# Loading the modulation weights and the first weight units between the two token halves of x

## The reference, cut to what matters

```
def rms_norm(x, g):
    x32 = x.astype(jnp.float32)
    y = x32 * lax.rsqrt(jnp.mean(x32 * x32, axis=-1, keepdims=True) + EPS)
    return (y * g.astype(jnp.float32)).astype(x.dtype)

def ada_params(cvec, w, b):
    m = jax.nn.silu(cvec) @ w + b
    return jnp.split(m, 3, axis=-1)

def modulate(x, g, shift, scale):
    return rms_norm(x, g) * (1.0 + scale) + shift
...
        shift, scale, gate = ada_params(c, ada_w[i], ada_b[i])
        ...
        h = modulate(x_lat, norm_g[i], shift[:, None, :], scale[:, None, :])
        ...
            proj = h @ w_in
```

## Time and profile before

| What | us |
|---|---|
| three runs | 2718.04, 2719.57, 2719.70 |
| median of the three | 2719.57 |
| the profiled execution | 2720.78 |
| its span in the profile, first to last instruction | 2718.8 |
| PE busy | 2655.6 (98%) |
| DVE busy | 1675.7 (62%) |
| ACT busy | 1017.9 (37%) |
| POOL busy | 1011.1 (37%) |

### The profile page before, as it was taken

One profiled execution on the slowest core, in us unless ns is written; L12 is line 12 of the kernel. 1 busy time (PEld: TensorE's weight loads), 2 busy tenths in 40 slices (PEclk: granted clock), 3 DMA queues, 4 the chain that ended last, 5 costly groups with the idle time before them and its releaser, 6 DMA issues.

```text
span 2718.8 us, 39199 instructions
## 1 busy us (share of the span) xinstructions
PE 2655.6 (98%) x16062; PEld 2189.9 (81%) x16062; DVE 1675.7 (62%) x1847; ACT 1017.9 (37%) x1392; POOL 1011.1 (37%) x612
## 2 busy tenths in 40 slices
PE   8999999999999999999999999999999999999997
PEld 5888878887788887788888888888777888888885
DVE  6496669867844457544556676666878443344446
ACT  4342247753433333544442223332334222222222
POOL 0254243114688853222121111111144654444552
PEclk9999999999999999999999999999999999999998
DMA  7211710034222232111121111111132111121112
GB/s 247 72 32 39 263 47 1 1 101 127 68 62 57 53 116 85 47 47 47 47 58 40 40 34 38 40 40 40 32 93 63 55 47 47 47 63 55 55 34 98
DMA packets 248541, 175.26 MB, mean 64 GB/s; under 512 B 6064, under 2 KB 236848, under 8 KB 247216
## 3 DMA queue, kind: packets, MB, share of 16 engines
q1 hardware_dynamic: 246928, 170.22, 20.3%
q10 hardware_dynamic: 1440, 2.59, 0.3%
HBM read 164.40 MB, written 8.39 MB: 64 GB/s over the span
## 4 chain that ended last, share of the span: by engine, by line
PE 68%; issue 13%; DVE 9%; POOL 4%; ACT 3%; DVEq 2%; SPq 1%; DMA 0%; POOLq 0%; ACTq 0%
PE PS L2619 10%; PE PS L2621 10%; PE PS L2620 10%; PE PS L2219 10%; PE PS L2221 9%; PE PS L2220 9%; POOL Wlo L629 3%; DVE qR L1709 2%; ACT exp L1070 1%; DVE acol L1757 1%; PE PS L2723 1%; PE PS L2730 1%; PE PS L2532 1%; PE PS L2808 1%; DVE qz L1713 1%
## 5 line engine op out<-in xcount | busy, mean ns | idle before, releaser
L629 POOL TENSOR_TENSOR Wlo<-Wraw,Whi 128x1024 fp32r<-128x1024 f32 (+1 forms) x140 | 342.0, 2443 | 989.1 <-ACT Whi L844 972.7
L2219 PE MATMUL PS<-Bh,Whi 128*128 128x512 f32 x1184 | 472.4, 399 | 6.3 <-DVE Bl L1501 2.8
L2221 PE MATMUL PS<-Bh,Wlo 128*128 128x512 f32 x1184 | 461.8, 390 | 0.0
L2220 PE MATMUL PS<-Bl,Whi 128*128 128x512 f32 x1184 | 461.2, 390 | 0.0
L2219 PE MATMUL PS<-Hh,Whi 128*128 128x512 f32 x672 | 266.0, 396 | 3.8 <-POOL Wlo L629 1.2
L2219 PEld LDWEIGHTS PS<-Bh,Whi 128*128 128x128 f32 x1184 | 222.1, 188 | 59.0 <-DVE Bl L1501 6.9
L2221 PE MATMUL PS<-Hh,Wlo 128*128 128x512 f32 x672 | 261.8, 390 | 0.0
L2221 PEld LDWEIGHTS PS<-Bh,Wlo 128*128 128x128 f32 x1184 | 222.2, 188 | 47.7
L2220 PEld LDWEIGHTS PS<-Bl,Whi 128*128 128x128 f32 x1184 | 222.5, 188 | 44.2 <-issue 0.7
L2220 PE MATMUL PS<-Hl,Whi 128*128 128x512 f32 x608 | 236.8, 389 | 0.0
L2166 DVE TENSOR_TENSOR X<-X,PS 128x1024 f32<-128x1024 f32 x56 | 68.3, 1221 | 204.7 <-PE PS L2621 203.9
(11 more groups left out here) (459 smaller groups left out, 5927.7 us busy)
## 6 DMA issues: line engine op xcount, KB each, us to landing
Wraw<-in_w_in SPq DMA_DIRECT2D x64, 512.0 KB, 4.0
adarow<-in_ada_rows SPq DMA_DIRECT2D x32, 512.0 KB, 6.8
Wraw<-in_odd_w_in SPq DMA_DIRECT2D x32, 512.0 KB, 5.0
Wraw<-in_w_up SPq DMA_DIRECT2D x32, 512.0 KB, 4.0
Wraw<-in_w_down SPq DMA_DIRECT2D x28, 512.0 KB, 4.2
Wraw<-in_even_w_in SPq DMA_DIRECT2D x24, 512.0 KB, 3.9
adaW<-in_ada_in SPq DMA_DIRECT2D x8, 1024.0 KB, 11.6
Wraw<-in_even_w_out SPq DMA_DIRECT2D x14, 512.0 KB, 3.6
```

Source lines behind the costliest of these rows:

```text
L629: pool.tensor_tensor(Wlo[:, slot, 0:tiles, :], Wraw[:, slot, 0:tiles, :], Whi[:, slot, 0:tiles, :].bitcast(F32), ALU.subtract).then_inc(lo ...
L2219: mm(out, Whi[:, u % 2, k, :], hi[:, k, c], start=(k == 0), stop=False)
L2220: mm(out, Whi[:, u % 2, k, :], lo[:, k, c], start=False, stop=False)
L2221: return mm(out, Wlo[:, u % 2, k, :], hi[:, k, c], start=False, stop=(k == KT - 1))
```

## The change

SP issues the first half of x, pieces 0 and 1, units 0 and 1, the second half of x, and then pieces 2 to 7. The other engines follow that order:

- ACT squares the first half only, takes its root (L926), copies the first rows, splits both units, and then squares the second half, two squares before each of the first two high parts.
- DVE inverts the first root, makes the first columns, tiles (0, 0) and (1, 0), and only then the second half's sums, its root, tiles (0, 1) and (1, 1), and the second columns.
- PE makes the products of tiles (0, 0) and (1, 0) before the second half's sum. That sum is four products instead of two, the last two squares going in without an addition. The second modulation rows follow, then product (0, 1), the second columns, product (1, 1).

The number of matmuls for `Hh` and `Hl` stays; six filler products go. `FIRST_HALVES` lists the new order of the halves. Context squares and the context's load wait for all six of the sum's products. From channel tile 2 on all is as before.

```diff
-        for h in range(2):
+
+        def x_half(h):
+
             c = slice(h * 512, h * 512 + 512)
...
-        unit_at(0, 0, w_in0)
-        for t in range(8):
-            if t == 2:
-                unit_at(1, P, w_in0)
...
+        x_half(0)
+        ada_piece(0)
+        ada_piece(1)
+        unit_at(0, 0, w_in0)
+        unit_at(1, P, w_in0)
+        x_half(1)
+        for t in range(2, 8):
+            ada_piece(t)
+        sp.wait_ge(sem("xsq_read"), 6)
...
+        for n in range(KT):
+            square_half(n)
+        x_roots(0)
         rows_out(0)
+        split(0, 0, 16)
         split(1, 1, 16)
+        for n in range(2):
+            square_half(KT + 2 * n)
+            square_half(KT + 2 * n + 1)
+            high_half(n)
+        for n in range(4, KT):
+            square_half(KT + n)
+        x_roots(1)
         act.dma_start(chan[:, :], nW["chan_dft"]).then_inc(sem("chan_loaded"), 16)
-        for j in range(4):
+        rows_out(1)
+        high_half(2)
+        high_half(3)
+        for j in range(1, 4):
...
+        def second_sum():
+
+            for n, tile in enumerate((4, 8, 10, 11)):
+                if n < 2:
+                    pe.wait_ge(sem("xsq_added"), n + 3)
+                else:
+                    pe.wait_ge(sem("xsq_ready"), n + 13)
+                mm(bank(5), ones, xsq[:, tile, :], start=(n == 0), stop=(n == 3)).then_inc(sem("xsq_read"), 1)
...
         modulation_columns(0)
         keep_running(3)
+        first_products(0, 0)
+        first_products(1, 0)
+        second_sum()
         modulation_rows(1, (0,))
         keep_running(4)
-        for j in range(1, 4):
+        modulation_rows(1, (1,))
+        first_products(0, 1)
+        modulation_columns(1)
+        first_products(1, 1)
+        for j in range(2, 4):
             first_products(2 * j - 2, 0)
-            modulation_rows(j, (1,) if j == 1 else (0, 1))
+            modulation_rows(j)
```

More of the change, by code:

```diff
@@ L282, in build @@
         (c0 + 1024, c0 + 1280, c0 + 2560, c0 + 3328, c0 + 3584, c0 + 3840, t0 + 52736))]
+    FIRST_HALVES = [(0, 0), (1, 0), (0, 1), (1, 1)] + [(k, h) for k in range(2, KT) for h in range(2)]
     ROWS = 6
@@ L904, in act_program, with square_half, x_roots @@
         act.activation(small[:, 8:10], bank(0, 2), ACT.Exp).then_inc(sem("act_setup"), 1)
-        for n in range(2 * KT):
+        def square_half(n):
             h, k = n // KT, n % KT
             act.wait_ge(sem(f"slot_loaded{4 * h + k // 2}"), 16)
-            if n == 12:
-                act.wait_ge(sem("xsq_read"), 1)
-            act.activation(xsq[:, n % 12, :], X[:, k, h * 512:h * 512 + 512], SQUARE).then_inc(sem("xsq_ready"), 1)
-        split(0, 0, 16)
-        for h in range(2):
-            act.wait_ge(sem("xsq_read"), 2 * h + 2)
+            if n == 8:
+                act.wait_ge(sem("xsq_read"), 2)
+            act.activation(xsq[:, k + 4 * h, :], X[:, k, h * 512:h * 512 + 512], SQUARE).then_inc(sem("xsq_ready"), 1)
+        def x_roots(h):
+            act.wait_ge(sem("xsq_read"), (2, 6)[h])
             act.activation(Rx[:, h * 512:h * 512 + 512], bank(4 + h), SQRT, bias=EPSC, scale=1.0 / D).then_inc(sem("x_root"), 1)
@@ L937, in act_program @@
             if k < 4:
-                act.wait_ge(sem("xsq_read"), 4)
+                act.wait_ge(sem("xsq_read"), 6)
             else:
@@ L1575, in scaled_half @@
         def scaled_half(n):
-            k, c = n // 2, slice(n % 2 * 512, n % 2 * 512 + 512)
+            k, h = FIRST_HALVES[n]
+            c = slice(h * 512, h * 512 + 512)
             stt(tnx[:, n % 4, :], X[:, k, c], A0[:, k:k + 1], Rx[:, c], ALU.mult, ALU.mult).then_inc(sem("x_tn"), 1)
         def low_half(n):
-            k, c = n // 2, slice(n % 2 * 512, n % 2 * 512 + 512)
+            k, h = FIRST_HALVES[n]
+            c = slice(h * 512, h * 512 + 512)
             dve.wait_ge(sem("x_hi"), n + 1)
@@ L1584, in add_fours @@
         def add_fours(n):
-            a = 4 * (n % 3)
+            a = 4 * min(n, 1)
             for b in (0, 2):
@@ L1590, in add_fours @@
             tt(xsq[:, a, :], xsq[:, a, :], xsq[:, a + 2, :], ALU.add).then_inc(sem("xsq_added"), 1)
-        for n in range(4):
-            add_fours(n)
+        add_fours(0)
+        add_fours(1)
         root_to_scale(0)
-        root_to_scale(1)
-        modulation_columns(0)
-        for j in range(4):
+        modulation_columns(0)
+        scaled_half(0)
+        scaled_half(1)
+        low_half(0)
+        low_half(1)
+        add_fours(2)
+        dve.wait_ge(sem("xsq_ready"), 14)
+        tt(xsq[:, 8, :], xsq[:, 8, :], xsq[:, 9, :], ALU.add).then_inc(sem("xsq_added"), 1)
+        root_to_scale(1)
+        scaled_half(2)
+        scaled_half(3)
+        low_half(2)
+        low_half(3)
+        modulation_columns(1)
+        for j in range(1, 4):
             n = 4 * j
@@ L2313, in pe_program @@
         keep_running(5)
-        for h in range(2):
-            for j in range(2):
-                n = 2 * h + j
-                if n:
-                    keep_running(2 if n == 1 else 3)
-                pe.wait_ge(sem("xsq_added"), n + 1)
-                mm(bank(4 + h), ones, xsq[:, 4 * (n % 3), :], start=(j == 0), stop=(j == 1)).then_inc(sem("xsq_read"), 1)
+        for n in range(2):
+            if n:
+                keep_running(2)
+            pe.wait_ge(sem("xsq_added"), n + 1)
+            mm(bank(4), ones, xsq[:, 4 * n, :], start=(n == 0), stop=(n == 1)).then_inc(sem("xsq_read"), 1)
+        def second_sum():
[5 more added lines that the diff above has]
+                mm(bank(5), ones, xsq[:, tile, :], start=(n == 0), stop=(n == 3)).then_inc(sem("xsq_read"), 1)
         def column_tiles(out, W, sem_done):
@@ L2342, in modulation_columns @@
                 pe.wait_ge(sem("m_ready"), j - 1)
-            if j == 0:
-                pe.wait_ge(sem("x_root"), 2)
+            if j < 2:
+                pe.wait_ge(sem("x_root"), j + 1)
             for t in range(2):
```

8 lines of the change are left out of this document (5 added, 3 removed).

## The result

| What | before, us | after, us |
|---|---|---|
| median of seven runs each | 2719.57 | 2728.11 |
| lowest and highest run | 2718.04, 2720.44 | 2725.28, 2735.61 |
| the profiled execution | 2720.78 | 2725.73 |
| its span | 2718.8 | 2723.8 |
| PE busy | 2655.6 | 2654.9 |

The changed kernel is slower by 0.36%: the ratio of the times is 1.0036, with a 95% interval of 1.0026 to 1.0045. The forecast was 2726.6 and the range 2721.5 to 2731.0. One slow run of the kernel before, of 14047.14 us, lies among those beside units_plain, rows_first, score_fill and rows_fill, and counts in no comparison.

A forecast was written before the change was run, and what follows sets the result against it. TensorE sets the time after the opening, so an opening delay reaches the end: 44.25 - 37.70 = +6.55 us, plus 0.5 for the clock, +7.05 on the 2719.57 median, giving 2726.6 us; range 2721.5 to 2731.

The forecast's parts named there:

- the mark: Start of the second modulation columns on DVE: 37.70 us before, 44.25 forecast; the kernel moves by what it moves.
- Landings: Opening transfers arrive in issue order: second half of x 9.5 us later, the modulation 7.3 us earlier, same total.
- First columns: First modulation columns reach DVE at 20.6 us instead of 28.49, 7.9 us ahead.
- The hold: POOL's low-part subtractions block DVE's scale operation and first scaled tile, which ends at 26.2 us instead of 22.1.
- rival 1: Opening: weight splits don't hold DVE, or come late enough; +3.7 us, total 2723.3, chance 0.19.
- The ping-pong and the second sum: DVE and ACT alternate on tiles and squares; PE's sum of the second half runs 31.6 to 35.3 us.
- From the sum to the mark: Second root 0.75, reciprocal 3.4, tile until 41.8, product group 1.4 and columns 1.0, reaching 44.25 us.
- Costed at nothing: Opening: rows of pieces 2 and 3, row copy, early products, later loads and removed fillers add 0 us.
- The clock: PE idles 5.6 us in the opening, then runs at half clock: +0.5; second fall taken as 0, 2.4 in range.
- rival 2: Opening: PE's lower clock stays or comes twice; +10.4 us, total 2730.0, chance 0.13.
- For 3: Rival: second root hidden, piece 3 sets the second columns at 35.2 us, 2.5 earlier; total 2717.1, chance 0.04.
- For 4: Rival: opening transfers share engines and land together, piece 1 and units up to 3 us later; about +10, chance 0.04.

The follow-up runs named there:

- units_plain: changed kernel with weight units 0 and 1 transferred ahead of modulation pieces 0 and 1, and ACT's splits ahead of root and rows; median 2731.98 us, ratio 1.0040.
- rows_first: kernel before with PE's modulation rows moved ahead of each round's first product in the loop over channel pairs; median 2719.87 us, ratio 0.9999.
- score_fill: kernel before with nine filler products on PE ahead of the attention stage's first ten transposes, near 382.5 us; median 2717.81 us, ratio 0.9994.
- rows_fill: kernel before with both the earlier modulation rows of rows_first and the attention-stage fillers of score_fill; median 2718.46 us, ratio 0.9994.
- fill_no_lock: changed kernel with fillers in PE's two idle stretches, and POOL writing zeros as low parts of units 0 and 1, left out of the product; median 2722.88 us.
- order_alone: kernel before with only SP's new order of transfers, the engines staying in the old order; median 2729.53 us, ratio 1.0036.
- engines_alone: changed kernel with the transfers back in the old order, so the engines' new order alone; median 2736.90 us, ratio 1.0059.
- fill: changed kernel with twelve instead of three fillers behind the first modulation columns and four behind piece 3's rows; median 2725.04 us, ratio 1.0026.
- no_lock: changed kernel with POOL writing zeros, reading nothing, as low parts of units 0 and 1, which the product leaves out; median 2724.52 us, ratio 1.0018.
- long_sum: fill with four more products of 512 columns ahead of the second half's sum, overwritten by it; median 2730.03 us, ratio 1.0038 to the kernel before.
- after_again: the changed kernel run once more with no edit, beside the kernel before; median 2727.78 us, ratio 1.0026.

## Why the prediction was right, point by point

- **What bounds, and the mark.** Right for the profiled execution, and not enough for the median. The mark moved by 6.19 us on the axis, 5.95 of it stood at 1245 us and 4.97 at the end. The medians of fill_no_lock and order_alone lie 3.6 and 10.0 above the kernel before, their marks 3.54 and 9.95 behind its own. But others don't fit as well: 8.5 for 6.83 in the changed kernel, 17.6 for 14.85 in engines_alone, 12.1 for 7.81 in units_plain. Behind the mark stand the fall at 386 us and the hold beside it, each in some executions only.
- **Landings.** Right in order and rate. First rows straight behind the sum, piece 1's rows at 17.11, unit 1's split at 20.31 and second-half squares at 21.67 are each 0.5 to 0.6 ahead of the prediction's axis (17.7, 20.9 and 22.2), as S is (0.64).
- **First columns.** 20.6 predicted, 19.96 measured: 6.58 after S, and 6.58 by the prediction.
- **The hold.** The mechanism and its size: 2.85 us were what the hold was worth in the sum (6.55 against rival 1's 3.7), 2.40 were measured by the pair fill and fill_no_lock. The first tile ended 0.5 behind POOL's splits (0.7 predicted), with 3.29 for the two tiles. With POOL only writing (no_lock) the hold was gone. The Trainium skill, "SBUF — State Buffer", section "Who interferes with whom", has a DVE instruction with two SBUF inputs and a GpSimd instruction that reads SBUF exclude each other; the traces agree, with 1.95 against 0.16 us for L1598.
- **The ping-pong and the second sum.** Sum predicted 31.6 to 35.3, measured 31.28 to 34.88. From S the start is 17.90 instead of 17.58, but two errors meet in it: without the lower clock it is 16.91 (fill), 0.67 less than summed, and the lower clock added 0.99. That the sum lies on the path, long_sum shows (3.43 for 3.6).
- **From the sum to the mark.** 12.65 predicted, 12.61 measured.
- **Costed at nothing.** Held: the rows of pieces 2 and 3 ran beside the reciprocal, the row copy was done at 39.62, ahead of the high part at 39.85.
- **The clock: the term that was mis-sized.** I took +0.5 for the first fall; it was 0.89 (30.51 against 29.62), and the low level lasted 6.8 us and not some 3. The sum without the clock was +6.55, and fill, without a fall in the opening, has +5.94. So I was 0.61 too high there and 0.39 too low for the clock, and that +7.05 came so near to the +6.83 from S is in part luck. I took 0 for a second fall, and kept 2.4 for the range. In the first changed execution it was 0; in after_again the mark was 2.63 later, 1.51 of it by the second fall and 1.12 by a later first one. That is rival 2's mechanism, with a chance of 0.13, and one of two profiled executions had it. The forecast for the like of the profiled execution (2727.8) was 2.1 too high: 0.9 of it on the axis at the mark (7.05 against 6.19, of which 0.64 is the earlier S), the rest given back behind it (6.19 to 4.97). That for the median (2726.6) was 1.5 too low. The step that failed is taking one execution's clock for the median's: the changed kernel's runs spread over 10 us, and the median stood 8.5 above the kernel before's, where the profiled execution stood 4.95 above.
- **Rivals 1, 3 and 4.** Rival 1 was wrong as a forecast and right as a price: fill_no_lock is that case, +3.54 against its +3.7. The prediction called that price no measurable difference; the interval of fill_no_lock, 1.0003 to 1.0021, is just clear of none. For 3, the second root was ready 7.7 us too late (inverted at 38.98, where 31.3 was needed). For 4, landings kept their order.
- **What stays open.** In the profiled executions of fill and units_plain DVE was held by POOL in the attention stage, 350 us behind the opening, and both then lost 5.4 us. What decides who is held, and whether a shift of the opening makes it more frequent, was not tried; that the changed kernel's highest runs (2732.46, 2735.61) come from it fits their distance, but they were not profiled. And no run counted how many executions have the second fall.

## What to carry to other kernels

Before a long step is moved earlier, follow what then comes last. Here the modulation came 8 us sooner, but the second half of x came 9.6 us later (its first squares 8.3 us after S instead of 1.35 ahead of it), and its chain of square, sum, root, reciprocal, tile and product, which had been hidden under the weights' transfer, became the opening's length: 3.5 us lost before any side effect. The side effects nearly doubled that: POOL's subtractions moved onto DVE's first two-input operations (2.4 us), and PE's longer waits (5.32 and 2.46 us) were followed by the half clock, the first in both profiled executions, the second in one of them (0.9 and 3.5 us). Profile a kernel in several executions when an idle time of PE near 2.5 us stands in it, or when a DVE operation of two inputs and a POOL subtraction start within hundredths of a microsecond of each other: here the second fall was worth 1.5 us at the mark between two executions of one program, and executions in which DVE was the one held lost 5.4 us.

## What the runs showed of the hardware that I had not expected

- The same idle time of PE does not always have the same consequence. After 2.58 us at 386 us the granted clock was 0.50 in the kernel before and 1.00 in rows_first; after 2.46 us in the opening it was 1.00 in the first execution of the changed kernel and 0.61 over the next 4 us in the second. And these two executions of one program changed places in the attention stage: after 2.58 us of idleness the first had 0.55 from 392 to 395 (below), the second 1.00 from 396 to 402.
- A fall lasted 6.8 us in the opening of the changed kernel, 3.8 of them with PE at work again in the first execution and 6.2 in the second; and in its attention stage, after the same 2.58 us as before, (0.45 + 0.12) x 3 / 0.5 = 3.4 us:

```profile
392.00:395.00 3.00, 2.38 (x7) 1.60 (x9) 1.75 (x3) 2.55 (x4) 2.86 (x2) 0.55 0.00 0
395.00:398.00 3.00, 3.00 (x21) 2.08 (x18) 2.20 (x5) 0.55 (x1) 2.86 (x3) 0.88 0.02 5
```

- Between POOL's two subtractions DVE got its turn, but for one operation only. The 256-number scale operation ended at 22.22, as the first of the two did (they start at 19.84 and take 4.66 together); the tile behind it ended near 25.0, 0.5 behind the second (24.50). POOL lost nothing: two subtractions took 4.66, and one took 2.35 at 19.68 in the kernel before, with no DVE operation of two inputs beside it.
- Which of the two is held differs with a few hundredths of a microsecond in their starts. With DVE 0.06 us ahead, at 399 us, they took 1.55 (DVE) and 4.29 (POOL); with POOL 0.01 ahead, in fill, 4.27 and 2.93 (the rows under fill). In the first order PE had no wait for DVE there; executions with the second lost some 5.4 us.
